# A decoder layer with a mixture of experts: a seventh place in SBUF for gate and up weights

## The reference

```python
def reference(x, c, ...):
    h = rms_norm(x, g_attn) * (1 + scale_a) + shift_a          # modulation row from silu(c) @ w_ada + b_ada
    o = concat(dsa_attention(...), diff_attention(...))        # top-256 sparse heads | differential heads
    x = x + gate_a * dot(o, w_out)
    h = rms_norm(x, g_moe) * (1 + scale_m) + shift_m
    y = hier_moe(h, ...)                                       # best of 4 groups, top 2 of its 8 experts
    return rms_norm(x + gate_m * y, g_final)

def hier_moe(h, ...):
    for e in range(32):
        hid = silu(dot(h, w_gate[e])) * dot(h, w_up[e])
        y = y + gates[:, e:e+1] * dot(hid, w_down[e])
```

## Time and profile before

| | us |
|---|---|
| median of 3 runs | 1015.45 (1013.06 to 1015.51) |
| the profiled execution's own time | 1012.76 |
| its span in the trace | 1010.9 |
| TensorE busy (PE) | 953.0, 94% |
| VectorE busy (DVE) | 593.9, 59% |
| ScalarE busy (ACT) | 400.2, 40% |
| GpSimd busy (POOL) | 118.4, 12% |

### The profile page before, as it was taken

One profiled execution on the slowest core, in us unless ns is written; L12 is line 12 of the kernel. 1 busy time (PEld: TensorE's weight loads), 2 busy tenths in 40 slices (PEclk: granted clock), 3 DMA queues, 4 the chain that ended last, 5 costly groups with the idle time before them and its releaser, 6 DMA issues.

```text
span 1010.9 us, 15051 instructions
## 1 busy us (share of the span) xinstructions
PE 953.0 (94%) x5352; PEld 519.3 (51%) x5352; DVE 593.9 (59%) x1593; ACT 400.2 (40%) x909; POOL 118.4 (12%) x218
## 2 busy tenths in 40 slices
PE   3899999999999999999999999999899999979974
PEld 2464575444448756677766455557433433323431
DVE  3389647999999798987777234366233332212226
ACT  6131236666650488777678021112212111111113
POOL 2000000000008411110000000000111111111004
PEclk9999999999999999999999999998999999989988
DMA  9997101110111000050000421199899999999978
GB/s 325 335 358 269 42 22 27 37 42 23 41 42 27 1 1 2 1 190 2 1 2 1 187 84 63 72 364 340 312 406 421 421 417 420 418 423 419 396 290 352
DMA packets 70957, 191.98 MB, mean 190 GB/s; under 512 B 10264, under 2 KB 37200, under 8 KB 58592
## 3 DMA queue, kind: packets, MB, share of 16 engines
q1 hardware_dynamic: 62896, 173.15, 44.9%
q0 software_dynamic: 5760, 16.78, 4.3%
q10 hardware_dynamic: 2224, 1.05, 0.4%
HBM read 173.12 MB, written 22.04 MB: 193 GB/s over the span
## 4 chain that ended last, share of the span: by engine, by line
PE 66%; DVE 20%; DMA 6%; issue 5%; ACT 1%; POOL 1%; SPq 1%; POOLq 0%; DVEq 0%; ACTq 0%
PE PS L2014 12%; PE PS L1891 11%; DVE BIAS L1157 8%; PE PS L2037 7%; PE PS L1784 6%; PE PS L1827 5%; PE PS L1849 4%; DMA X<-in_w_down_dram 3%; PE PS L1745 3%; PE PS L1697 3%; PE PS L1844 2%; DVE X L1221 2%; PE PS L1722 2%; PE PS L2001 2%; PE PS L1662 2%
## 5 line engine op out<-in xcount | busy, mean ns | idle before, releaser
L1697 PE MATMUL PS<-HT,X 128*128 128x512 f32 x384 | 168.8, 593 | 0.0
L2014 PE MATMUL PS<-QKV,HT 128*32 128x512 f32 (+2 forms) x640 | 129.0, 603 | 1.8 <-ACT HT L966 1.7
L1697 PEld LDWEIGHTS PS<-HT,X 128*128 128x128 f32 x384 | 72.5, 190 | 92.4 <-issue 92.2
L870 ACT ACTIVATE X<-X,nmx 128x128 f32<-128x128 f32 (+7 forms) x128 | 98.4, 770 | 51.7 <-DVE nmx L1221 51.5
L1891 PE MATMUL PS<-QKV,HT 128*128 128x512 f32 x256 | 113.7, 597 | 0.0
L1157 DVE TENSOR_SCALAR_CACHE_REDUCE BIAS<-SC,tk 128x384 f32<-128x384 f32 (+3 forms) x128 | 96.4, 809 | 1.1
L1509 DVE TENSOR_TENSOR HT<-PS,HT 128x256 f32<-128x256 f32 x20 | 8.5, 424 | 149.5 <-ACT HT L974 149.5
L853 ACT ACTIVATE X<-SC,tk 128x896 f32<-128x896 f32 x64 | 69.6, 1088 | 43.1 <-DVE tk L1145 43.1
L1784 PE MATMUL PS<-QKV 64*128 64x512 f32 (+3 forms) x384 | 79.0, 517 | 1.6 <-DVE nmx L1221 1.1
L1891 PEld LDWEIGHTS PS<-QKV,HT 128*128 128x128 f32 x256 | 47.4, 190 | 53.7 <-issue 53.6
L2037 PE MATMUL PS<-QKV,HT 128*32 128x512 f32 (+2 forms) x320 | 67.1, 613 | 2.2 <-DMA X<-in_w_down_dram 2.2
(11 more groups left out here) (298 smaller groups left out, 1502.0 us busy)
## 6 DMA issues: line engine op xcount, KB each, us to landing
QKV<-in_w_gate_dram SPq DMA_DIRECT2D x22, 1024.0 KB, 16.7
QKV<-in_w_up_dram SPq DMA_DIRECT2D x22, 1024.0 KB, 20.8
QKV<-in_w_down_dram SPq DMA_DIRECT2D x22, 1024.0 KB, 26.3
QKV<-in_w_ada_dram SPq DMA_DIRECT2D x8, 2048.0 KB, 14.0
QKV<-in_w_ada_dram SPq DMA_DIRECT2D x8, 1024.0 KB, 12.7
X<-in_w_in_dram SPq DMA_DIRECT2D x16, 512.0 KB, 3.8
QKV<-expert_rows SPq DMA_DIRECT2D x16, 512.0 KB, 10.4
X<-in_w_gate_dram SPq DMA_DIRECT2D x5, 1024.0 KB, 16.7
```

The source lines that it names most:

```text
L870: act.activation(sc, sc, ACT.Exp, bias=nmx[:, i % 4, m:m + 1], scale=-1.0, accum_out=rs[:, i, m:m + 1]).then_inc(exp_done, 1)
L1697: end = pe.matmul(PS[:, 2 * b + half, :], WS[:, b, j, :], HT[:, j, BANK * half:BANK * (half + 1)], start=(j == 0), stop=(j == KC - 1))
L2014: end = pe.matmul(PS[at, 2 + b, :], hgT[b][:, P * c_ + at.start:P * c_ + at.stop], WGU[w][:, c_, :, :], start=(c_ == 0), stop=(c_ == KC - 1))
```

## The change

The scratch that the compiler reserves in each SBUF partition for the descriptors of dynamic DMAs goes from its default of 16384 bytes to 2048. With it, and with the columns of arrays that only routing and attention use (`mrows`, `rs`, `iw`, `tk`, and `lst` and `dst_rows`, which move into unused columns of SC), a new tile W7 of 4096 columns is made. Gate and up weights get seven places (`GUS` = 7), down weights keep six (`DNS` = 6), and which columns hold which place changes. The hand-written list ahead of step 0 and the two refill rules follow. Two semaphores are merged into one (`w_in_out`), and the small `diag` tile moves to SC.

```diff
-    RING = 6
+    GUS = 7
+    DNS = 6
...
+        W7 = sb("W7", [P, 4 * S])
...
+        mrows = W7[0:3 * KC, 0:P]
+        rs = W7[:, P:P + 2 * NA].rearrange("p (i m) -> p i m", m=2)
+        iw = W7[:, 2 * P:2 * P + T * IH].rearrange("p (t h) -> p t h", t=T)
+        tk = W7[:, 3 * P:3 * P + 6 * NS].bitcast(U32).rearrange("p (a n) -> p a n", a=6)
+        lst, dst_rows = (SC[:, 4 * S + NT * i:4 * S + NT * (i + 1)].bitcast(I32) for i in range(2))
...
-        homes = [QKV[:, 0:6144], QKV[:, 6144:12288], X[:, 0:6144], QKV[:, 12288:18432], QKV[:, 18432:24576]]
-        gu_at = [a[:, 0:4096] for a in homes[0:4]] + [homes[4][:, 2048:6144], SC[:, 0:4096]]
-        dn_at = [a[:, 4096:6144] for a in homes[0:4]] + [homes[4][:, 0:2048], BIAS[:, 0:2, :].rearrange("p a n -> p (a n)")]
+        gu_at = [QKV[:, 0:4096], QKV[:, 6144:10240], QKV[:, 20480:24576], W7[:, :], X[:, 0:4096],
+                 QKV[:, 12288:16384], SC[:, 0:4096]]
+        dn_at = [QKV[:, 4096:6144], QKV[:, 10240:12288], X[:, 4096:6144], QKV[:, 18432:20480], QKV[:, 16384:18432],
+                 BIAS[:, 0:2, :].rearrange("p a n -> p (a n)")]
...
                     sp.wait_ge(op_sb, 2 * EARLY)
-                    gate_up_load(sp, expert_of(RING - 2), RING - 2)
+                    for w in range(IN_X, IN_X + 2):
+                        gate_up_load(sp, expert_of(w), w)
...
-            for w in range(IN_X, IN_X + 2):
-                if w == IN_X + 1:
-                    store_h2(SPILLED)
-                    sp.wait_ge(op_ps, 2 * T)
-                gate_up_load(sp, expert_of(w), w)
-                if w == IN_X + 1:
-                    store_h2(T - 1)
+            gate_up_load(sp, expert_of(4), 4)
+            down_load(sp, expert_of(2), 2)
+            store_h2(SPILLED)
+            sp.wait_ge(op_ps, 2 * T)
+            gate_up_load(sp, expert_of(5), 5)
+            store_h2(T - 1)
+            for w in range(3, 5):
                 down_load(sp, expert_of(w), w)
...
-            gate_up_load(sp, expert_of(RING - 1), RING - 1)
+            gate_up_load(sp, expert_of(6), 6)
...
-            for w in range(RING - 2, RING):
-                down_load(sp, expert_of(w), w)
+            down_load(sp, expert_of(5), 5)
...
-                    for w in freed(n):
-                        gate_up_load(sp, expert_of(w), w % RING)
+                    for w in freed(n, GUS):
+                        gate_up_load(sp, expert_of(w), w % GUS)
...
-                    for w in freed(n - 1):
-                        down_load(sp, expert_of(w), w % RING)
+                    for w in freed(n - 1, DNS):
+                        down_load(sp, expert_of(w), w % DNS)
...
-    nc = _bacc.Bacc("TRN2", target_bir_lowering=False, num_devices=1)
+    nc = _bacc.Bacc("TRN2", target_bir_lowering=False, num_devices=1, dynamic_dma_scratch_size=2048)
```

More of the change, by code:

```diff
@@ L321, in hybrid_layer @@
         out_row_in, modc_set = sem("out_row_in"), sem("modc_set")
-        wi_in, ws_in = sem("wi_in"), [sem(f"ws_in{i}") for i in range(2)]
+        w_in_out, ws_in = sem("w_in_out"), [sem(f"ws_in{i}") for i in range(2)]
         lam_ready, lam_exp, op_sb = sem("lam_ready"), sem("lam_exp"), sem("op_sb")
@@ L354, in hybrid_layer @@
         oh_done, route_done = sem("oh_done"), sem("route_done")
-        gu_in = [sem(f"gu_in{i}") for i in range(RING)]
-        dn_in = [sem(f"dn_in{i}") for i in range(RING)]
+        gu_in = [sem(f"gu_in{i}") for i in range(GUS)]
+        dn_in = [sem(f"dn_in{i}") for i in range(DNS)]
         xg_in = [sem(f"xg_in{i}") for i in range(2)]
@@ L536, in expert_of, with freed @@
                 return sp.value_load(eid[0:1, SEQ[w]:SEQ[w] + 1], min_val=0, max_val=NE - 1)
-            def freed(n):
-                return [w for w in range(RING, NE) if last_use[w - RING] == n]
+            def freed(n, places):
+                return [w for w in range(places, NE) if last_use[w - places] == n]
             for t in range(SPILLED):
@@ L1893, in project_out @@
                 end.then_inc(op_ps, 1)
-            pe.wait_ge(wo_in, 16)
+            pe.wait_ge(w_in_out, 32)
             def choose(q):
@@ L2039, in down_proj, with weights_of @@
                     end.then_inc(dn_ps, 1)
-            def weights_of(n):
-                return ([(w % RING, g, size) for w, g, size in parts[n]],
-                        sorted({(w % RING, 16 * (w // RING + 1)) for w, _, _ in parts[n]}))
+            def weights_of(n, places):
+                return ([(w % places, g, size) for w, g, size in parts[n]],
+                        sorted({(w % places, 16 * (w // places + 1)) for w, _, _ in parts[n]}))
             turn_rows(0, 0, 16)
-            gate_up(0, 0, *weights_of(0))
+            gate_up(0, 0, *weights_of(0, GUS))
             turn_rows(1, 1, 16)
@@ L2066, in _ @@
                             turn_rows(n, over(b), i * 16 + 16 * (uses(over(b)) + 1))
-                            arrived = i * 16 + 16 * (len(range(b, NE, RING)) + 1)
-                            gate_up(n, over(b), [(b, 0, 4)], [(b, arrived)])
+                            came = lambda places: i * 16 + 16 * (len(range(b, NE, places)) + 1)
+                            gate_up(n, over(b), [(b, 0, 4)], [(b, came(GUS))])
                             turn_hidden(n, over(b))
-                            down_proj(n, over(b), [(b, 0, 4)], [(b, arrived)])
+                            down_proj(n, over(b), [(b, 0, 4)], [(b, came(DNS))])
             def add_into(i, stationary, rows, start, stop):
```

24 lines of the change are left out of this document (9 added, 15 removed).

## The result

| us | before | changed |
|---|---|---|
| median of the runs | 1014.46 (1012.37 to 1016.13) | 1020.22 (1017.82 to 1022.29) |
| span of the profiled execution | 1010.9 | 1018.7 |

The ratio is **1.0055 (1.0042 to 1.0067)**: slower by 5.8 us. The forecast was 1019.0 with a range of 1010.0 to 1022.5; sign and range held, the size of the loss was put at 3.5.

What follows compares the result with a forecast made beforehand. DMA and TensorE were both near their limit. A 5.9 us late start, 11.3 of old waits gone, and 7.2 wait plus 1.75 clock at down_proj(15) gave +3.5: 1016.3 profiled, 1019.0 median, range 1010.0 to 1022.5.

Steps and rivals of the forecast that it cites:

- wait at down_proj(15): Expert stage: down weights of w = 25 land at 926.5, TensorE comes at 919.3, so it waits 7.2 us.
- end of down_proj(15) later by: Expert stage: after its wait down_proj(15) loses 1.75 to the clock and ends 3.5 us later than before.
- The start: Step 0: first gather takes 9.0 us beside a full queue, and TensorE's first product ends 5.9 us late.
- The first rival: Step 0: gather is not held up and lands after 4.6 us; head start 9.0, profiled time 1013.1; chance 0.22.
- 1.0 us of cover: Ahead of the first gather: the token list covers 6.0 us, so a last h2 store 5.0 us later leaves 1.0.
- 3.1 us of head start are left: Before the full DMA stretch: of 5.0 us, 3.1 remain for every load with the same bytes ahead.
- The order of the queue: SyncE's refills: down weights from w = 6 to 27 have 2 MB more ahead and land 1.9 us later.
- the stage's end, the last scatter and the read-back move by the same 3.5: Behind down_proj(15): no later step waits, so everything to the end shifts by 3.5 us.
- the offset that it used: Final sum: the profiled execution was taken as 2.7 us under the median, 1012.76 against 1015.45.
- The head start comes through whole: Expert stage: both old waits go, nothing replaces them, and 5.0 us of data come off; 1010.4; chance 0.13.
- The smaller scratch blocks GpSimd: Expert steps: a gather waits for the scatter ahead, 18 us a pair, +108 over 20 steps, 1123; chance 0.03.
- a wait at gate_up(15) "as now": Sign against the forecast: waits there as in the kernel before (5.45 us) would say the head start was lost.

Runs made afterwards that it cites:

- e2: Changed kernel with gate and up weights of w = 6 and down weights of w = 4 held until both first gathers landed, ahead of a modulation row; ratio 1.0063.
- e5: Changed kernel with gate and up weights of w = 6 and down weights of w = 4 held until both first gathers landed, behind the modulation row; ratio 1.0029.
- e9: Changed kernel with loads of w = 2 and 3 behind the tile 5 stores, and refills in order of need from turn 6; ratio 0.9978.
- e3: Changed kernel with down refills ahead of gate and up refills in each turn of SyncE's loop; ratio 1.0048.
- e12: Changed kernel with only the refills changed, issued from turn 6 on in the order in which TensorE needs them; ratio 1.0015.
- e8: Changed kernel with seven places, but gate and up refills issued in the turns of the kernel before; ratio 1.0049.
- e1: Kernel before with the scratch of 2048 bytes and nothing else changed; 1013.95 us, ratio 0.9998.
- e11: Kernel before (six places) with the load of w = 4 behind the tile 5 stores and refills in order of need from turn 6; ratio 0.9992.
- e7: Changed kernel with loads of w = 2 and 3 behind the tile 5 stores, and down refills first in each turn; ratio 1.0041.
- e6: Changed kernel with gate and up loads of w = 2 and 3 behind the stores of residual tile 5 and h2 tile 5; ratio 1.0020.

## Why the prediction was right in sign and short in size

| step of the prediction | predicted | measured |
|---|---|---|
| store of residual rows lands later by | 5.0 | 4.8 (t = 31.2 for 26.4) |
| first gather, issue to landing | 9.0 | 10.0 |
| turn_rows(0) later by | 4.0 | 4.5 |
| gate_up(0) longer by | 1.9 | 1.6 |
| head start left at 24 MB | 3.1 | 0.0 |
| wait at down_proj(12) | none | 2.18 |
| wait at gate_up(15) | none | 1.19 |
| wait at down_proj(15) | 7.2 | 5.47 |
| end of down_proj(15) later by | 3.5 | 8.9 |
| from the last step to the end | unchanged | 3.0 shorter |

The measured column goes by t.

**The start.** The mechanism was right: the gather is slow beside a full queue (9.98), and 4.6, 4.5 and 5.0 in e2, e5 and e9, where the queue runs empty. The first rival, that it isn't held up, falls. The 1.0 us of cover that was to be left was gone in this execution: the last h2 store landed at 708.9 and released the gather at 709.85, where VectorE had written the token list from 708.20 on. By t the store was not late (51.7, with 52.4 predicted); the token list came 1.3 us earlier than in the kernel before. In e3 and e12, with the same list ahead of step 0, the token list released the gather, it took 8.6, and TensorE waited 3.7, near the 4.0 of the prediction. The prediction left out that TensorE can also transpose at the low clock after its idle time, 1.94 in place of 1.04 by the order of time. The first product ended at 732.25, t = 75.1, where it ended at t = 68.1 before. The loss at the start is 7.0 us, where I had 5.9: 4.5 until turn_rows(0), 0.9 more until gate_up(0), and 1.6 in it. The three experiments with the same start end that product at t = 74.9 (e3), 74.5 (e8) and 75.5 (e12), so the lateness belongs to the kernel and not to one execution.

**The step that failed: "3.1 us of head start are left".** What SyncE's queue had moved (packets, MB, share of 16 engines), counted from 650, up to t = 65, 80 and 91.5 of the kernel before:

```profile
q1 hardware_dynamic: 3171, 19.95, 74.8%
...
q1 hardware_dynamic: 3921, 25.47, 77.7%
...
q1 hardware_dynamic: 4445, 29.27, 78.6%
```

and of the changed kernel:

```profile
q1 hardware_dynamic: 3456, 22.55, 78.5%
...
q1 hardware_dynamic: 3862, 25.09, 74.0%
...
q1 hardware_dynamic: 4442, 29.29, 75.9%
```

At t = 65 the changed kernel is ahead by 2.6 MB, the whole two loads and a little. Fifteen microseconds later it is behind by 0.4, and at t = 91.5, where the first 24 MB have landed in the kernel before, both are level. The prediction had the second half of w = 7 landing at 737.1, t = 82.1; it landed at 733.75 + 7.6 = 741.4, t = 84.2. Of these 2.1 us, 1.1 are the late product, 0.3 the issue and 0.7 the landing; the last 1.0 of the 3.1 came with w = 8. The shares of the windows above tell the same. The gap from 718 to 740 leaves out 6 x 0.55 + 6 x 0.25 + 10 x 0.42 = 9.0 us of full rate, the old one from 710 to 718 left out 8 x 0.46 = 3.7. The difference of 5.3 is close to the 5.0 us that the two loads had brought forward; the windows are not aligned by t, so it is the counts that show it.

**The order of the queue.** This term held in direction: e12, which changes nothing else, removes all three waits at down_proj and is worth 4.0 us. Its size was set by the head start. The weights of down_proj(15) were predicted for 926.5, t = 271.5, and landed at 933.15, t = 276.0: 4.4 later, of which 3.1 are the missing head start. The bytes tell most of the other 1.3. From the moment when both kernels are level (746.47 and 748.67) to this landing (922.56 and 933.15), SyncE's queue moves 62.46 MB before and 64.70 now, and the queue of the rows 11.33 and 12.43. These are 3.3 MB more, where the prediction had 2.10 + 0.84 = 2.9; the difference is 0.9 us. The rest fits the rate, 419 GB/s in place of 420 over 180 us. For want of the head start down_proj(12) and gate_up(15) kept 2.2 and 1.2 of their waits, and TensorE came to down_proj(15) at 927.7, t = 270.5, where the prediction had 919.3, t = 264.3, so that the wait itself was shorter than predicted. Behind it down_proj(15) took 6.21, where I had 5.3. From here the end of down_proj(15) is 939.36, t = 282.2, 8.9 later than the t = 273.3 of before: 3.5 predicted, 4.4 for the landing and 0.9 for the clock.

**The step that hid half of this: "the stage's end, the last scatter and the read-back move by the same 3.5".** They did not. The last scatter of the kernel before, from its chain:

```profile
969.03 5.70 DMA expert_rows<-HT,dst_rows
```

It takes 3.30 in the changed kernel (chain above), which is 2.4 of the 3.0. In the kernel before, TensorE waits at that time for residual rows, whose loads are behind the last weights on SyncE's queue:

```profile
973.52 9.55 PE L2075 MATMUL PS<-X,ident 128*128 128x512 f32 x16 [6.02 <-DMA X<-residual_rows]
```

In the changed kernel they are there, and TensorE goes on without a wait:

```profile
978.21 3.70 PE L2077 MATMUL PS<-X,ident 128*128 128x512 f32 x8
```

The experiments split the same way. Where TensorE waits 5.6 to 5.9 for residual rows (e1, e8 to e12), the last scatter takes 5.3 to 5.6 in the four whose chain shows it (e1, e8, e11, e12); where it waits 0.2 or not at all (e2 to e7), 3.3 to 4.3. I read this as a scatter beside a busy queue against one beside a free queue: with the last steps later for TensorE than for the DMA, the residual rows are in before it. No experiment moved those six loads, so this reading stays argued.

So two misses of opposite sign stand in the sum: by the last step the kernel is 8.6 late, not 3.5, and 3.0 of it come back. That the forecast of 1019.0 lies only 1.2 from the median is in part luck: besides these two misses, 1.0 of the offset that it used was the spread of the three runs on record, and with 1014.46 as the median of before it would have been 1018.0.

**The rivals.** "The head start comes through whole" falls with the queue's count. "The smaller scratch blocks GpSimd" falls with e1. "The gather is not held up" fell above. Of the signs that the prediction named, a wait at gate_up(15) "as now" was to tell that the head start was lost; it was lost, and the wait was 1.2 all the same, since TensorE itself came late.

## What to carry to other kernels

Here an extra buffer brought transfers forward and put back everything behind them on the same queue: before adding one, look which store or small gather on the path to the next stage now stands behind or beside it, and move that ahead. When one kind of operand gets more buffers than another, refills by "what came free" no longer match the order of need, and issuing them by need was worth as much as the start. A lead in bytes is real only if it is still there when the full stretch begins, so count the queue's bytes at that moment rather than at the moment of issue.

## What the hardware showed that I had not expected

- The idle time ahead of step 0 costs twice over: after 5.7 us of waiting the granted clock was 0.50 from 718 to 724 and 0.77 from 724 to 730 (2.4 GHz is 1.00, 1.2 GHz 0.50), and transposes and product took 2.5 us more than before. In e12 gate_up(0) took 9.77 behind a wait of 3.7, here 8.69 behind 5.7, and in e9 8.81 with no wait for the gather (granted clock 0.72 from 718 to 724), where the kernel before took 7.12. So the length of the wait alone does not tell the price, and a gather in time does not always save it.
- Behind the wait at down_proj(15) the whole product ran near the low level, 0.58, and took 6.21 for 3.57:

```profile
933.10:939.40 6.30, 6.25 (x33) 0.58 1.03 422
```

- The first gather, of 128 rows, takes 4.5 to 5.0 us where SyncE's queue runs empty (e1, e2, e5, e9), 6.7 in e6 and 6.4 in e7, and 8.6 to 10.0 where the queue is full (e3, e8, e12 and the changed kernel). The Trainium skill's rule in "DMA: Bandwidth & Descriptors", section on queues, rings and completion order, that the engines take turns between queues packet by packet, would leave it about half of the bandwidth: for its 0.5 MB at 417 GB/s some 1.2 us more, an estimate, where the runs show 4 to 5. These runs do not agree with that for the whole gather; what holds it up, the packets or the issue of its descriptors, was not tried.
- The 40 indirect DMAs with a scratch an eighth as large ran at the same speed (e1: ratio 0.9998).
